# Second block's attention: work beside the softmax taken in another order, weight splits last, a third bank for the latent keys

## The reference

```python
proj = rms_norm_2(x, attn_norm[l]) @ w_in[l]
h_mla, h_diff, h_ch = jnp.split(proj, [IN_MLA, IN_MLA + IN_DIFF], axis=-1)
o_mla  = rms_norm_2(mla_attention(h_mla, ...), mla_out_norm[l])
o_diff = diff_attention(h_diff, ...)          # normalised per head inside
o_ch   = rms_norm_2(chunk_attention(h_ch, rel_bias[l]), chunk_out_norm[l])
x = x + jnp.concatenate([o_mla, o_diff, o_ch], axis=-1) @ w_out[l]
x = x + conv_ffn_2(rms_norm_2(x, ffn_norm[l]), ...)
```

## Time and profile before

| | |
|---|---|
| median of 3 runs | 1713.27 us (1712.95 to 1716.1) |
| profiled execution | 1714.17 us, its span 1712.9 us |
| TensorE busy | 1596.4 us, 93% of the span |
| VectorE, ScalarE, GpSimd busy | 1052.8, 808.1, 239.6 us |
| mean granted TensorE clock | 0.974 |

### The profile page before, as it was taken

How to read it: one execution, slowest core, us unless ns; L and a number is a source line. 1 busy time by engine, 2 the same in 40 slices (tenths; PEclk the granted TensorE clock), 3 DMA queues, 4 the chain that set the end, 5 groups by cost and what they waited for, 6 DMA issues and landing times.

```text
span 1712.9 us, 26858 instructions
## 1 busy us (share of the span) xinstructions
PE 1596.4 (93%) x10834; PEld 1383.6 (81%) x10834; DVE 1052.8 (61%) x1923; ACT 808.1 (47%) x1514; POOL 239.6 (14%) x284
## 2 busy tenths in 40 slices
PE   5899979999999999979899997888999998899998
PEld 3788758877777788867799986777999887689996
DVE  3633765465344434688677767566676656667765
ACT  1322962442233323448455553555555545555553
POOL 1200330011010100013011101142111011321110
PEclk8999999999999999989999998899999998999999
DMA  9466013163564224030346453323455533245452
GB/s 377 157 255 260 18 60 123 75 246 123 206 261 172 76 96 147 26 123 2 130 169 217 174 187 118 133 91 131 165 180 180 204 126 124 74 148 191 179 206 77
DMA packets 39418, 257.27 MB, mean 150 GB/s; under 512 B 5504, under 2 KB 6784, under 8 KB 10496
## 3 DMA queue, kind: packets, MB, share of 16 engines
q1 hardware_dynamic: 36416, 249.61, 39.9%
q0 software_dynamic: 1296, 4.72, 0.8%
q10 hardware_dynamic: 1584, 1.23, 0.3%
HBM read 254.49 MB, written 1.05 MB: 149 GB/s over the span
## 4 chain that ended last, share of the span: by engine, by line
PE 81%; DVE 9%; ACT 6%; issue 2%; DMA 1%; POOL 1%; SPq 0%; ACTq 0%; DVEq 0%
PE ps L473 24%; PE ps L474 23%; PE ps L475 23%; PE ps L489 2%; PE ps L615 2%; PE ps L637 2%; PE ps L624 2%; DVE wl L1677 1%; ACT wh L1253 1%; ACT arena L1589 1%; PE ps L1019 1%; PE ps L515 1%; DMA raw<-in_ev_w_in 1%; ACT arena L1324 1%; PE ps L599 1%
## 5 line engine op out<-in xcount | busy, mean ns | idle before, releaser
L1677 DVE TENSOR_TENSOR wl<-raw,wh 128x1024 fp32r<-128x1024 f32 (+2 forms) x328 | 383.1, 1209 | 393.6 <-ACT wh L1253 393.1
L1253 ACT CAST wh<-raw 128x1024 fp32r<-128x1024 f32 (+1 forms) x338 | 333.4, 1036 | 532.9 <-PE ps L475 402.9
L473 PE MATMUL ps<-xh,wh 128*128 128x256 f32 (+1 forms) x1582 | 495.4, 313 | 8.4 <-ACT arena L1546 8.1
L474 PE MATMUL ps<-xl,wh 128*128 128x256 f32 (+1 forms) x1582 | 490.0, 310 | 0.0
L475 PE MATMUL ps<-xh,wl 128*128 128x256 f32 (+1 forms) x1582 | 490.0, 310 | 0.0
L473 PEld LDWEIGHTS ps<-xh,wh 128*128 128x128 f32 x1582 | 303.4, 192 | 33.3 <-issue 9.2
L473 PE MATMUL ps<-wh,xh 128*128 128x512 f32 (+2 forms) x844 | 305.9, 362 | 20.0 <-DVE xl L2227 6.8
L475 PEld LDWEIGHTS ps<-xh,wl 128*128 128x128 f32 x1582 | 303.4, 192 | 15.3
L474 PEld LDWEIGHTS ps<-xl,wh 128*128 128x128 f32 x1582 | 303.5, 192 | 15.1 <-issue 0.7
L475 PE MATMUL ps<-wh,xl 128*128 128x512 f32 (+2 forms) x844 | 301.3, 357 | 0.0
L474 PE MATMUL ps<-wl,xh 128*128 128x512 f32 (+2 forms) x844 | 301.2, 357 | 0.0
(11 more groups left out here) (208 smaller groups left out, 1791.1 us busy)
## 6 DMA issues: line engine op xcount, KB each, us to landing
raw<-in_ada SPq DMA_DIRECT2D x48, 1024.0 KB, 6.8
raw<-in_up SPq DMA_DIRECT2D x44, 1024.0 KB, 6.1
raw<-in_fin SPq DMA_DIRECT2D x44, 1024.0 KB, 4.8
raw<-in_down SPq DMA_DIRECT2D x22, 1024.0 KB, 4.8
raw<-in_fout SPq DMA_DIRECT2D x22, 1024.0 KB, 4.8
raw<-in_win SPq DMA_DIRECT2D x12, 1024.0 KB, 4.9
raw<-in_ev_w_in SPq DMA_DIRECT2D x9, 1024.0 KB, 7.6
raw<-in_wout SPq DMA_DIRECT2D x8, 1024.0 KB, 4.8
```

The lines of the kernel that those rows point to most:

```text
L473: e.matmul(out, A[0], B[0], start=first, stop=False)
L474: e.matmul(out, A[0], B[1], start=False, stop=False)
L1253: e.copy(hi_of(j)[:, a:b], raw_of(j)[:, a:b]).then_inc(*S.hi.up((j, half)))
L1677: e.tensor_tensor(lo_of(j)[:, a:b], raw_of(j)[:, a:b], hi_of(j)[:, a:b].bitcast(F), ALU.subtract).then_inc(*S.lo.up((j, half)))
```

## The change

- `ON_POOL` loses win9 of both layers: its low part is made by VectorE, in `beside(6)`, and no longer by GpSimd at i = 6. GpSimd keeps wout2 at i = 8.
- `beside` on both engines takes the turned block first, then the copies, and the weight split last.
- VectorE normalises units 6 to 10 right after their factors, ahead of `turned` and `softmax(i)`; units 0 to 5 stay behind `softmax(i)`.
- `up_keys` takes fixed banks: kn0, kn1, kn2 in 6, 7, 4 and vm0, vm1 in 6, 7. It calls `bank()` no more, so the two later banks are dealt out in the opposite order from then on.

```diff
-    ON_POOL = {SPLITS[0]} | {J[k] for k in (("win0", 9), ("win1", 9), ("wout0", 2), ("wout1", 2), ("fin0", 1), ("fin1", 1))}
+    ON_POOL = {SPLITS[0]} | {J[k] for k in (("wout0", 2), ("wout1", 2), ("fin0", 1), ("fin1", 1))}
...
-                for g in range(3):
-                    b = bank()
+                for g, b in enumerate((6, 7, 4)):
                     wait_bank(b)
...
-                for t in t2:
-                    b = bank()
+                for t, b in enumerate((6, 7)):
                     wait_bank(b)
...
             def beside(i):
-                if i in (1, 2, 3, 4, 6, 8, 10):
-                    weights(after({1: J[win, 5], 2: J[win, 6], 3: J[f"uq{l}", 0], 4: J[f"ukv{l}", 0], 6: J[win, 7],
-                                   8: J[win, 8], 10: J[win, 9]}[i]))
+                if i in TURN:
+                    g = TURN[i]
+                    q.wait_ge(*S.tr.at(("turned", l, g)))
+                    high(("y", l), 3 + g, ps[BANK.get(("turned", l, g), 0)], vec("mix", 8 * l + 3 + g, 1))
...
-                if i in TURN:
-                    g = TURN[i]
-                    q.wait_ge(*S.tr.at(("turned", l, g)))
-                    high(("y", l), 3 + g, ps[BANK.get(("turned", l, g), 0)], vec("mix", 8 * l + 3 + g, 1))
+                if i in (1, 2, 3, 4, 6, 8, 10):
+                    weights(after({1: J[win, 5], 2: J[win, 6], 3: J[f"uq{l}", 0], 4: J[f"ukv{l}", 0], 6: J[win, 7],
+                                   8: J[win, 8], 10: J[win, 9]}[i]))
...
             def beside(i):
-                if i in (1, 2, 3, 4, 10):
-                    weights(after({1: J[win, 5], 2: J[win, 6], 3: J[f"uq{l}", 0], 4: J[f"ukv{l}", 0], 10: J[win, 9]}[i]))
+                if i in TURN:
+                    g = TURN[i]
+                    low2(("y", l), 3 + g, ps[BANK.get(("turned", l, g), 0)], vec("mix", 8 * l + 3 + g, 1))
...
-                if i in TURN:
-                    g = TURN[i]
-                    low2(("y", l), 3 + g, ps[BANK.get(("turned", l, g), 0)], vec("mix", 8 * l + 3 + g, 1))
+                if i in (1, 2, 3, 4, 6, 10):
+                    weights(after({1: J[win, 5], 2: J[win, 6], 3: J[f"uq{l}", 0], 4: J[f"ukv{l}", 0], 6: J[win, 7],
+                                   10: J[win, 9]}[i]))
...
                 if 0 <= i - 1 < A.n:
                     factors(i - 1)
+                    if i > 6:
+                        normalise(i - 1)
...
-                if 0 <= i - 1 < A.n:
+                if 0 <= i - 1 < 6:
                     normalise(i - 1)
...
-                if i in (6, 8):
-                    weights(after(J[win, 4 + i // 2]))
+                if i == 8:
+                    weights(after(J[win, 8]))
```

## The result

The changed kernel takes 1720.41 us (median of 6 runs, 1719.78 to 1723.38) against 1714.26 us of the kernel before on the same chip (6 runs, 1712.95 to 1717.23): ratio 1.0036, 95% interval 1.0023 to 1.0049. It is slower by 0.36%. The prediction was 1703.2 us, 0.6% faster, with a range of 1699 to 1709.5. The profiled execution took 1721.09 us, its span 1719.8 us. The later runs were made on several chips, so their times are compared by the ratio to the kernel before on the same chip.

What follows compares the result with a forecast made beforehand. TensorE, busy 93% of the span, was taken as the bound. Gains of 5.05 us per layer, 10.1 over two, took the profiled 1714.17 us to 1704.1, or 1703.2 on the median's scale; range 1699 to 1709.5.

Steps and rivals of the forecast that it cites:

- step 4: After up_keys: column(7, 0) runs 24 products at full clock, 2.9 us in place of up to 4.8.
- the port rival: Steps 9 and 10: GpSimd's wout2 low part may block normalise(8), out 1.3 to 2.4 us later per layer; chance 0.15.
- step 2: up_queries: uq copies no longer behind ukv's cast; up_queries ends at 1097.95, exp(3) at 1100.55, still late.
- The third rival: Late splits put cast, low part and maximum in series, costing a further 1.5 to 2.5 us per layer; chance 0.15.
- steps 1, 3 and 6: Splits of uq, win7 and win9, where late splits might cost a further 1.5 to 2.5 us per layer.
- step 10: Turned block before wout1's split: low2 of y5 ends at 1148.15, out("d", 0) starts 5.1 us earlier.
- The sign of being wrong: Clock 0.50 in steps 5 to 10, normalise(8) over 2 us, or out("d", 0) less than 3 us earlier after exp(1).
- step 1: Copy before uq's split: up_queries waits for the low part, exp(2) moves from 1092.99 to 1094.4, a 1.4 us loss.
- the first rival: Seven short pauses hold the clock at 1.2 GHz in steps 1 to 10; decides from about 8 us; chance 0.06.

Runs made afterwards that it cites:

- e13: Changed kernel plus unread matmuls in five TensorE pauses: before up_queries, vm0, column(7, 0), second half of transposes(8), out("d", 0); 1713.27 us, ratio 0.9988.
- e1: Changed kernel with out("d") multiplying its blocks in the order 4, 5, 3 instead of 3, 4, 5; 1712.27 us, ratio 0.9988.
- e2: Changed kernel with the weight split of uq put back ahead of the copy in step 1 only; 1714.48 us, ratio 1.0000.
- e5: Changed kernel plus 24 unread matmuls in TensorE's wait before out("d", 0); 1713.18 us, ratio 0.9987.
- e9: Kernel before, nothing moved, plus unread matmuls in two waits: 16 before kn2, 24 before out("d", 0); 1708.79 us, ratio 0.9959.
- e14: e3 plus unread matmuls before vm0, column(7, 0), second half of transposes(8) and the feed-forward entry transposes; 1702.64 us, ratio 0.9934.
- e12: Changed kernel plus 10 unread matmuls before up_queries; 1720.78 us, ratio 1.0028.
- e11: e3 plus 22 unread matmuls before the transposes that open the feed-forward; 1706.59 us, ratio 0.9938.
- e8: Kernel before with the turned block ahead of wout1's split in step 10 alone, and out("d") in block order 4, 5, 3; 1714.20 us, ratio 0.9993.
- e4: Kernel before with only the fixed banks 6, 7, 4 and 6, 7 in up_keys; 1720.71 us, ratio 1.0036.
- e3: Changed kernel with uq's split first again in step 1 and out("d") in block order 4, 5, 3; 1705.73 us, ratio 0.9955.

## Why the prediction was wrong

**The steps that held.** kn2's wait is gone, vm0 waits 1.34 us (1.55 forecast), column(7, 0) 1.44 (1.4), exp(2) starts at 1095.23 (forecast 1094.4, and everything here is shifted by the 0.87 us by which scores(0) came later), step 4 runs at 1.00. scores(8), at 1132.45, is 1.6 us behind its forecast with that shift; 1.3 of those are the clock's, since with the pauses filled (e13) it stands 50.05 us after scores(0) instead of 51.38. normalise(6) takes 0.67 us (0.5 to 0.8), against 2.32 beside GpSimd's low part. normalise(8) takes 0.55 and ends just before GpSimd's 4.72 us begin, so the port rival did not come true. Here the rule of the Trainium skill ("SBUF — State Buffer", Who interferes with whom), that whoever issues first has the shared port for the whole instruction, agrees with the trace: 0.55 us in front of GpSimd's instruction, 2.32 us inside one.

**The step that failed first: "out("d", 0) starts at 1148.25", right behind low2 of y5, with the cast and low part of wout1 counted as hidden under it.** The low part is not hidden, it is an operand. With block 3 last (e1) the wait has the forecast's size, 1.51 us. I read `out`'s moving operand and not its chunk index. In the kernel before the trace could not show it: wout1's split came first there, so this wait never ended last. Its price is 3.0 us at out("d", 0) (72.83 against 69.86), of which 1.22 come back as the wait of block 3. Of the 4.8 us by which out("d", 0) missed its forecast, 3.0 are this chunk, 1.3 the clock in step 2 (e13: 71.53), and 0.5 stay open. The third rival had late splits in it, but named steps 1, 3 and 6; the one that cost was step 10's. The sign of being wrong that the prediction gave, an `out` less than 3 us earlier, came (0.3 us, counted from scores(0)).

**The step that failed second: the clock, put at nothing in the sum and at a chance of 0.06 among the rivals.** I priced the pauses I added at their length, and let the clock decide only from 8 us of added work. The chain after the change shows what the pause in step 2 really is: copy, cast, a wait for its low part, and then products at 0.21 us.

```profile
1091.14 0.48 ACT arena L1544
1091.62 1.48 ACT wh L1251 x2
1093.09 1.22 issue
1094.31 0.54 PE ps L473
```

The 1.4 us of step 1, which I did forecast, cost 2.8 (e2), and the 4.49 us pause cost 2.45 on top (e5). Together, against e13, the clock takes 3.8 us from the changed kernel in the first layer and 4.3 in the second: half of the 8 that the rival asked for, and enough together with the late chunk. Two new slow stretches replaced the one that was removed.

**What it came to.** With the clock out of play in both, the kernel before stands at 100.6 us (e9) and the changed one at 103.0 (e13): the new order by itself, late chunk included, *loses* 2.4 us per layer. The clock costs 4.1 us in the one and 4.0 in the other. So 2.1 and 2.5 us per layer were lost in the profile, 4.6 in all, and the rest of the 6.9 us of profile against profile lies outside the attention: 0.9 ahead of it, 1.0 between the layers, 0.4 behind. My 5.05 us of gain per layer held, to four fifths, the 4.1 us of one slow stretch; the first rival counted what that stretch "gives back" as some 3 us beside the 5.1, though the steps had already been added up at full clock. Even with both mistakes mended and the pauses filled (e14) the order is worth only 0.5 us per layer over e9. Two readings were off as well, without weight in the sum: TensorE waits three times for normalise and not twice, and of the 15 matmuls at 1110 to 1113 the first few are narrower than 256 columns; one of 256 takes 0.21 us there.

My sum was right to count step 4 at full clock again. It was wrong to treat that as a gain that the same edit could not lose elsewhere. The Trainium skill ("TensorE: Matmul & The Clock Gate", A second HAM failure mode: psum-queue depth-cycling) says that short pauses between groups of matmuls can make the clock swing. The runs agree: behind pauses of 1.50 us (changed), 1.44 us (e12) and 1.67 us (e11) the clock went down, and with the pauses filled (e13) it did not. But the clock was not held down from steps 1 to 10, as the rival drawn from it had it: a short pause that was hit cost about 1.4 us, the long one of 4.49 us cost 2.45.

## What to carry to other kernels

Before a wait is called gone, list for the waiting instruction every operand with its chunk index, and give each its new time; the trace of before only shows the one that came last. Where TensorE is the bound, price a pause twice, its length and the slower products behind it, and ask first what the kernel would take with its pauses filled: e9 shows in one run that the clock had 4.1 us per layer to win; against it this order, mended, won 0.5. Another order may win more: e8's two edits brought the entry 1.2 to 1.3 us earlier with the slow stretch still there, and e8 and e9 together were not run. Matmuls that nobody reads, put into the pauses that cannot be removed, are then a fix of their own: 0.4% on the kernel before, untouched otherwise. e12 is the warning: with one pause filled and the others left, the clock fell behind another.

## What was not expected of the hardware

A pause of 1.50 us was enough for a clock of 0.54 behind it. It came after eleven small matmuls of transposes and scores, and the work behind it ran at 0.21 us a product for 3.3 us. A pause of 1.34 us before vm0 in the same profile left 1.00.

The same pause of 3.40 us before out("d", 0) leaves 1.00 in both layers of the kernel before and 0.50 to 0.61 in e4, in both layers. What decides between them stays open: no run here moved this pause alone by small steps.

A profile's slow stretches are one draw of several. e3 and e11 have the same instructions up to the entry of the first layer, and the same pause of 1.44 us before column(7, 0). Behind it e3's profile has 1.00 (first row) and e11's 0.71 (second row):

```profile
1107.00:1110.00 3.00, 3.00 (x28) 2.50 (x26) 1.40 (x5) 2.77 (x10) 1.07 (x2) 1.00 0.73 303
1110.00:1114.00 4.00, 4.00 (x27) 3.50 (x26) 0.97 (x4) 2.35 (x6) 1.02 (x1) 0.71 0.49 205
```

Runs of the kernel before spread from 1712.2 to 1720.1 us on one chip, with a mean clock of 0.978 or 0.979 in the shortest and 0.966 to 0.973 in the longest. The 0.966 of the longest is that of e4, so they may have e4's slow stretch behind `out`; no such execution was profiled.
